# A hybrid attention and recurrence step on one core: the first stage taken by groups of three row tiles and blocks of 128 features

## What is computed

```python
def rmsnorm(x, g):
    xf = x.astype(jnp.float32)
    y = xf * lax.rsqrt(jnp.mean(xf * xf, axis=-1, keepdims=True) + EPS)
    return (y * g.astype(jnp.float32)).astype(x.dtype)

def project(x, g_in, w_in, w_alpha_up, b_alpha):
    xn = rmsnorm(x, g_in)
    h = xn @ w_in
    ...
    log_a = jax.nn.log_sigmoid((ga @ w_alpha_up + b_alpha).astype(jnp.float32)) / GLA_TAU
```

## Time and profile before

| | us |
|---|---|
| median of 3 runs (960.92 to 961.86) | 961.21 |
| the profiled execution, its own time | 960.3 |
| its span in the trace | 958.5 |
| PE busy | 928.7 |
| DVE busy | 477.3 |
| ACT busy | 354.3 |
| POOL busy | 121.6 |

### The profile page before, as it was taken

One profiled execution on the slowest core, in us unless ns is written; L12 is line 12 of the kernel. 1 busy time (PEld: TensorE's weight loads), 2 busy tenths in 40 slices (PEclk: granted clock), 3 DMA queues, 4 the chain that ended last, 5 costly groups with the idle time before them and its releaser, 6 DMA issues. The chain is left out here.

```text
span 958.5 us, 16698 instructions
## 1 busy us (share of the span) xinstructions
PE 928.7 (97%) x6742; PEld 855.3 (89%) x6742; DVE 477.3 (50%) x1086; ACT 354.3 (37%) x847; POOL 121.6 (13%) x210
## 2 busy tenths in 40 slices
PE   7999999999999999999999999999998999999997
PEld 6999989999999899999989989988997989888884
DVE  6532166651215666234563455356456775991223
ACT  6444344432334444234442444335335332430011
POOL 1001033310102222000000000000001102540000
PEclk9999999999999999999999999999999999999999
DMA  8011111313111202350232101221124225551222
GB/s 288 26 48 44 45 46 46 91 46 97 44 41 28 61 23 69 96 181 10 67 136 72 52 22 46 72 73 46 45 69 134 77 82 157 174 181 44 88 88 77
DMA packets 85934, 75.12 MB, mean 78 GB/s; under 512 B 3665, under 2 KB 78050, under 8 KB 85602
## 3 DMA queue, kind: packets, MB, share of 16 engines
q1 hardware_dynamic: 85858, 74.05, 25.2%
HBM read 54.32 MB, written 19.73 MB: 77 GB/s over the span
## 5 line engine op out<-in xcount | busy, mean ns | idle before, releaser
L1371 PE MATMUL proj_bank<-x_hi,w_hi 128*128 128x352 f32 x1080 | 358.9, 332 | 1.3 <-DVE w_lo L615 1.3
L1373 PE MATMUL proj_bank<-x_hi,w_lo 128*128 128x352 f32 x1080 | 348.4, 323 | 0.0
L1372 PE MATMUL proj_bank<-x_lo,w_hi 128*128 128x352 f32 x1080 | 347.8, 322 | 0.0
L1371 PEld LDWEIGHTS proj_bank<-x_hi,w_hi 128*128 128x128 f32 x1080 | 204.5, 189 | 3.6 <-issue 2.3
L1372 PEld LDWEIGHTS proj_bank<-x_lo,w_hi 128*128 128x128 f32 x1080 | 204.7, 190 | 0.0
L1373 PEld LDWEIGHTS proj_bank<-x_hi,w_lo 128*128 128x128 f32 x1080 | 203.6, 189 | 0.0
L615 DVE TENSOR_TENSOR w_lo<-w_raw,w_hi 128x1024 fp32r<-128x1024 f32 x50 | 61.2, 1223 | 81.3 <-ACT w_hi L611 81.3
L963 ACT ACTIVATE probs<-score_banks,softmax_stats 128x128 f32<-128x128 f32 (+8 forms) x72 | 51.3, 715 | 77.8 <-DVE softmax_stats L1287 69.0
L1031 POOL TENSOR_TENSOR stats<-stats,minus_half 128x1 f32<-128x1 f32 (+1 forms) x36 | 22.3, 621 | 371.3 <-DVE stats L1320 371.3
L1016 POOL TENSOR_TENSOR decays<-log_decay 128x128 f32<-128x128 f32 (+1 forms) x122 | 47.6, 423 | 168.0 <-ACT log_decay L908 168.0
L611 ACT ACTIVATE w_hi<-w_raw 128x1024 fp32r<-128x1024 f32 x53 | 55.9, 1055 | 14.7 <-PE proj_bank L1373 14.7
(11 more groups left out here) (178 smaller groups left out, 1400.9 us busy)
## 6 DMA issues: line engine op xcount, KB each, us to landing
w_raw<-in_w_in SPq DMA_DIRECT2D x45, 512.0 KB, 4.4
merge_tanh_scratch<-feature_stage SPq DMA_DIRECT2D x16, 528.0 KB, 3.0
feature_stage<-merge_tanh_scratch SPq DMA_DIRECT2D x10, 528.0 KB, 3.9
x_rows<-in_x_prompt SPq DMA_DIRECT2D x8, 512.0 KB, 8.4
w_raw<-in_w_out SPq DMA_DIRECT2D x8, 512.0 KB, 4.6
branch_out<-in_x_prompt SPq DMA_DIRECT2D x8, 512.0 KB, 3.7
out<-branch_out SPq DMA_DIRECT2D x8, 512.0 KB, 2.6
tokens_stage<-merge_tanh_scratch SPq DMA_DIRECT2D x6, 528.0 KB, 3.5
```

The costliest lines, as they stand in the source:

```text
L1371: nc.tensor.matmul(out, wh, xh, start=first, stop=False)
L1372: nc.tensor.matmul(out, wh, xl, start=False, stop=False)
L1373: return nc.tensor.matmul(out, wl, xh, start=False, stop=last)
```

## The change

Four things change in the first stage and one behind it.

- **The norm gain.** It is no longer broadcast over the partitions. It is loaded as 8 rows of 128 numbers, transposed on PE to one column per block of features (`gain`), and applied later, as a scale per partition, when ACT copies the transposed block to `x_hi` and when DVE makes `x_lo`. `xn` becomes a multiply by one scalar per row (TENSOR_SCALAR).
- **Groups and blocks.** Row tiles are transposed in groups of three (384 columns, or 288 in the last group). A bank now holds one block of 128 features of a whole group, so there are 24 banks filled instead of 18, each of three transposes. The group is just the third of the rows (and 32 to 64 more) that a unit reads, and a unit's matmuls of block k wait for block k alone.
- **The `ga` tile.** Only its 16 columns are loaded. High and low parts stand side by side as one stationary operand of 32 columns, and a block takes two matmuls instead of three, 16 per unit. The results are two partial sums of 16 rows, and `w_alpha_up` is loaded twice, so that the small product (now 33 rows) adds them.
- **The small product.** Its nine matmuls go in pieces of three: `rank0` in the middle of unit 1,2, `rank1` behind it, the last piece (`la`) behind the first unit of `gq`. `la2`, `la3` and the first `gE` each move one unit back with it.
- **The recurrence.** At the first chunk of each j the unit that stood between `gL` and the next chunk's `gE` now stands behind that `gE`.

The matmuls on zeros between the first tiles are gone; the first 24 stay. The loads of x1 and x2 now stand ahead of the gain's, and w1 ahead of x3.

```diff
+X_ORDER = """sq0 ms0 xn0 sq1 ms1 sq2 ms2 xn1 xn2 gain hi0 hi1 lo0 xt0,0 xt0,1 xt0,2 xt0,3 lo1 sq3 ms3 unit0,0,0
+ xt0,4 xt0,5 xt0,6 xt0,7 sq4 xn3 ms4 sq5 ms5 unit0,0,1 unit1,0,0 xn4 sq6 xn5 ms6 sq7 unit1,0,1
+ xt1,0 xt1,1 xt1,2 xt1,3 xn6 ms7 sq8 ms8 unit0,1,0 xt1,4 xt1,5 xt1,6 xt1,7 xn7 xn8 unit0,1,1 unit1,1,0
+ xt2,0 xt2,1 xt2,2 xt2,3 unit1,1,1 xt2,4 xt2,5 xt2,6 xt2,7 unit0,2,0 unit0,2,1 lam split2 unit1,2,0 rank0 unit1,2,1 rank1"""
...
             stages.append(("gL", j, c))
             if c:
                 stages.append(("gN", j, c - 1))
-            if c == 0:
-                unit(*fill[c].pop(0))
             if c + 1 < NTT:
                 stages.append(("gE", j, c + 1))
...
+                    nc.scalar.activation(XH[:, k, cols], SC[:, b % 4, 0:cols.stop - cols.start], ACT.Copy,
+                                         scale=gain[:, k:k + 1]).then_inc(s_xh, 1)
...
-                    nc.vector.scalar_tensor_tensor(out=r[0:n, :], in0=r[0:n, :], scalar=stat[0:n, 32 + i % 2:33 + i % 2],
-                                                   in1=gin[0:n, :], op0=ALU.mult, op1=ALU.mult).then_inc(s_xn, 1)
+                    nc.vector.tensor_scalar(r[0:n, :], r[0:n, :], stat[0:n, 32 + i % 2:33 + i % 2], None,
+                                            ALU.mult).then_inc(s_xn, 1)
...
+                    nc.vector.scalar_tensor_tensor(out=XL[:, k, cols], in0=SC[:, b % 4, 0:cols.stop - cols.start],
+                                                   scalar=gain[:, k:k + 1], in1=XH[:, k, cols].bitcast(F),
+                                                   op0=ALU.mult, op1=ALU.subtract).then_inc(s_xl, 1)
...
+                    pe.wait_ge(s_xn, XG[q][-1] + 1)
+                    if b >= 4:
+                        pe.wait_ge(s_xl, b - 3)
...
-                        if t < 2:
-                            pe.wait_ge(s_xl, 2 * min(-(-TH * (th + 1) // P), NTT))
...
+                        if t < 2:
+                            pe.wait_ge(s_xl, KD_ * th + k + 1)
+                        if t == 0:
+                            both = GAW[:, k, :, :].rearrange("p b n -> p (b n)")
+                            nc.tensor.matmul(bank[0:2 * RANK, :], both, XH[:, k, cols], start=k == 0, stop=False)
+                            last = nc.tensor.matmul(bank[0:2 * RANK, :], both, XL[:, k, cols], start=False, stop=k == KD_ - 1)
+                            continue
```

More of the change, by code:

```diff
@@ L177, in stage_list @@
     for what in X_ORDER.split():
-        if what.startswith("unit"):
-            t, th = what[4:].split(",")
-            stages.extend(("unit", int(t), int(th), half) for half in range(2))
-        elif what.startswith("split"):
-            stages.append(("split", int(what[5:])))
-        else:
-            stages.append((what[0:2], int(what[2:])) if what != "lam" else ("lam",))
-    stages.append(("la",))
+        name = what.rstrip("0123456789,")
+        stages.append((name,) + tuple(int(v) for v in what[len(name):].split(",") if v))
     for n, u in enumerate(part["first"][6:]):
         unit(*u)
-        if n < 2:
-            stages.append(("la2",) if n == 0 else ("la3",))
-        elif n == 4:
+        if n < 3:
+            stages.append((("la",), ("la2",), ("la3",))[n])
+        elif n == 5:
             stages.append(("gE", 0, 0))
@@ L691, in _ @@
             sp.dma_start(g["CM"][:, :], a["c_coarse_mask"]).then_inc(s_gconst, 16)
[L692 to L693 removed]
+            for part in range(2):
+                sp.dma_start(g["WU"][RANK * part:RANK * (part + 1), :], a["w_alpha_up"][0, :, :]).then_inc(s_gconst, 16)
+            sp.dma_start(g["WU"][2 * RANK:2 * RANK + 1, :], a["b_alpha"]).then_inc(s_gconst, 16)
             for st in stages:
                 kind = st[0]
[L696 to L697 removed]
+                if kind == "split" or kind == "lo" and st[1] == 1:
+                    if st[1] < NW - 1:
                         load_w(st[1] + 1)
@@ L844, in _ @@
                             act.wait_ge(s_gateset, 1)
-                        nc.scalar.activation(g["GA"][0:RANK, cols], bank[0:RANK, :], ACT.Copy).then_inc(s_uout, 1)
+                        nc.scalar.activation(g["GA"][0:2 * RANK, cols], bank[0:2 * RANK, :], ACT.Copy).then_inc(s_uout, 1)
                     elif tk == "gk":
```

116 lines of the change are left out of this document (55 added, 61 removed).

## The result

| us | before | after |
|---|---|---|
| median of 4 runs | 961.54 (960.92 to 962.04) | 953.85 (952.91 to 954.33) |
| profiled execution, its span | 960.3, 958.5 | 954.33, 952.5 |
| landmark, start of the fourth feature tile | 67.82 | 63.80 |
| first chunks' `gL` of the recurrence | 116.62, 128.61 | 113.43, 124.01 |
| attention, the row that stood at 493.01 | 493.01 | 486.76 |

The ratio is 0.9919, with a 95% interval of 0.9902 to 0.9936. The kernel is faster, by 7.7 us at the median and 6.0 in the profiled execution, where 12.3 were forecast. 953.85 lies above the range of 945.8 to 953.3, by 0.6. The gain depends on the executions compared: over all its runs on record the kernel before takes 960.0 to 964.9 us, at a mean clock of TensorE from 0.995 down to 0.988, and the profiled one, from which the forecast was made, is among the fastest.

What follows compares the result with a forecast made beforehand. PE was taken to set the time. 10.7 us less at the landmark, minus 1.0 for the clock, plus 2.6 in the recurrence gave 12.3: 960.3 becomes 948.0, median 0.9 above, 948.9; range 945.8 to 953.3.

Steps and rivals of the forecast that it cites:

- I take 3.2, nearer to the upper end: First loads: without the gain's load ahead, what follows lands 3.2 us earlier, bounds 1.3 and 3.9.
- Two such multiplies end at about 10.7: Start: two of DVE's `xn` at 0.76 us each end at about 10.7, and PE's transposes start then.
- Rival 2: Start: w1 lands at 12.5, first `x_lo` at 14.0, time 951.2; or `xn` keeps 1.28, 949.9; chance 0.10.
- a refill 0.2: Group 0: refilling the banks between its two sets of four blocks costs 0.2 us.
- The charge of 1.0 for one stretch: Groups 0 and 1: one stretch of PE at the low clock costs 1.0 us; none to four are the ends.
- Rival 1: Groups 0 and 1: clock stays low, three or four slow stretches add 2 to 3.5 us: 951.7; chance 0.17.
- From there PE is fed: Behind group 1: group 2's transposes 2.4, unit 0,2 2.55 and unit 1,2 3.85 follow, from 28.8 to 41.4.
- It took 4.19: Small product, before `gq`: it keeps its nine matmuls and its earlier time of 4.19 us.
- nothing: Decay chain: moving `la2`, `la3` and first `gE` one unit keeps five units between them, so costs nothing.
- 24 matmuls fewer are 3.8: `ga` tile: two matmuls a block instead of three save 24 matmuls, 3.8 us.
- Rivals 3 and 4: First stage: no slow stretch, early loads, faster blocks, down to 946.1 (chance 0.08); blocks going round singly, 970.7 (0.04).
- Rival 5: PE comes early to something with its own time, constants' or weight loads; gain taken back, 959 to 961; chance 0.03.

Runs made afterwards that it cites:

- e5: The changed kernel again, unchanged: 952.02 us, ratio 0.9887.
- e10: The kernel before without the broadcast load of the norm gain, a tile of ones in its place: 959.82 us, ratio 0.9973.
- e15: The changed kernel with `xn1` ahead of `ms2` and 11 more matmuls on zeros behind the gain's transpose: 951.40 us, ratio 0.9879.
- e16: e12 run again, unchanged: 950.02 us, ratio 0.9863.
- e4: The changed kernel with DVE's multiply `xn1` ahead of `ms2`: 952.34 us, ratio 0.9894.
- e9: The changed kernel with the `ga` tile as before (whole w0 load, 128 stationary columns, three matmuls a block): 956.53 us, ratio 0.9937.
- e1: The changed kernel with 18 more matmuls on zeros behind the gain's transpose: 952.93 us, ratio 0.9900.
- e12: The changed kernel with `xn1` first, 11 more zero matmuls, group 2's small transposes last, last small-product piece between the next unit's halves: 949.15 us, ratio 0.9864.
- e2: The changed kernel with group 2's 32-row transposes behind the 128-row ones in each four blocks: 951.77 us, ratio 0.9891.
- e7: The changed kernel with `la`, `la2`, `la3` and first `gE` in old places, last small-product piece right behind `rank1`: 953.24 us, ratio 0.9895.
- e8: The changed kernel with the small product whole behind unit 1,2, and `la`, `la2`, `la3`, `gE` in old places: 951.58 us, ratio 0.9881.

## Why the prediction was right in direction and wrong in size

Twelve us were forecast for the profiled execution and six came; by the medians the forecast was 948.9, and 953.85 and 952.02 (e5) were measured. The second of these lies inside the range, so by how little it was missed is chance. The errors below are the same in both traces. The landmark was to be at 57.1 and one slow stretch charged with 1.0, so 58.1; it came at 63.80. By the forecast's own milestones:

| | forecast | measured | late |
|---|---|---|---|
| `x_rows1` lands | 6.6 | 7.68 | 1.1 |
| first `x_lo` | 11.7 | 13.88 | 1.1 more |
| unit 0,0 ends | 17.7 | 21.20 | 1.3 more |
| group 1 ends | 28.8 | 32.56 | 0.3 more |
| unit 1,2 ends, `rank0` taken out | 41.4 | 47.47 | 2.3 more |
| landmark | 57.1 | 63.80 | 0.6 more |

**The loads.** The step "I take 3.2, nearer to the upper end" failed. e10 shows 2.4 and after 2.1, within the bounds of 1.3 and 3.9. The argument from 184 GB/s between 5 and 6 us was no price. The landing itself differs by 1.6 us between executions, which the range should have held: of fourteen, eleven came at 7.60 to 8.26, one at 7.19 and two (e15, e16) at 6.64 and 6.74, as forecast. w1 came at 11.28 instead of 9.6: 1.2 by x2, the rest by the small load, which took 0.85 where the forecast had 0.3. It cost nothing, as ACT was ready for the first `x_hi` 0.9 before PE was.

**The start.** `xn` at 0.76 was right (0.75). "Two such multiplies end at about 10.7" left out that the power between them runs beside the first: 0.4 (e4). Of the rest, 0.35 is the low clock at the first block and 0.3 handovers. Rival 2, late by 2.3 through w1, gave the right lateness (14.0 for the first `x_lo`) by the wrong mechanism, which is luck; w1 wasn't what PE waited for. With a whole w0 ahead of it, w1 did hold up the first `x_hi`, by 0.7 (e9).

**Group 0.** The distance of 0.53 was right: four `x_lo` took 2.19 in e4 and e15. What failed is "a refill 0.2": the second four transposes stand on PE behind the half unit, which at 0.50 ended at 17.29, and DVE waited 0.99. With the clock at 1.00 that wait is 0.35 (e15).

**The clock.** The charge of 1.0 for one stretch was nearly right: 0.35 + 1.0 in after. Its reason was not: the fall came with PE's idle time ahead of group 0, 4.1 us in after, and not with the blocks and their handovers, since group 1 has the same and kept 1.00, and so did group 0 in e1, e12 and e15. Rival 1's three or four stretches never came. The rule beside it (the Trainium skill, "TensorE: Matmul & The Clock Gate", section "HAM oscillation — how this bites in real kernels") says that bursts behind waits can start at the low clock. The trace agrees for the burst behind 4.1 us and for none of those behind waits of 0.34 to 0.46.

**From there PE is fed.** This step had the largest error: 14.9 us instead of 12.6. "Transposes 2.4" is the term that failed: it was priced by 16 large ones in a row, 0.104 each, but 32-row transposes between 128-row ones cost more than large ones. To the next matmul's start they took 2.12 twice, 4.2 in all, which is 1.8 of the 2.3. The other 0.4 to 0.5 is in the handovers between transposes, products and `rank0` (the distance of matmuls there is 0.26 and not 0.16), for which no term stood. Putting the small ones last gives 1.1 back (e2). The forecast's 3.85 for a unit is right (21.20 to 25.07 is 3.87), although 24 x 0.159 is 3.82.

**The small product.** That pieces keep the clock was right (e7, e8). "It took 4.19" was not: 4.58, and 0.2 more around each piece.

**Moving `la2`, `la3` and `gE`: "nothing".** This failed by 0.85. The five units between the chain and `gE` were counted, but not what is queued behind `la3` on ACT: a weight split and PE's next copy. What stands behind the waiting instruction was looked at for the recurrence and not here.

**The recurrence.** Right: the two waits went, 2.8 to 2.95 for a forecast of 2.6.

**The ga tile.** The part "24 matmuls fewer are 3.8" is 2.4 by e9's trace, since in the groups the third matmul nearly fits into `x_lo`'s distance. The milestones didn't rest on it. The forecast for busy PE did, and it also took the waits inside the groups for idle time, which the records count as busy.

**Together:** 1.1 + 1.1 + 1.3 + 0.3 + 2.3 + 0.6 less the 1.0 charged for the clock, plus 0.85 for `la3`, less 0.35 for the recurrence, is 6.2; the profiled execution was 6.3 above the 948.0. Rivals 3 and 4 did not happen. Rival 5's mechanism exists in a place it did not name: ACT's copy. The range failed because every step of one chain was taken at its likely value, and nearly all of them erred late.
